# Narrow feed-forwards of a one-core transformer pair: order of one weight split, place of the rotary tables, and a first weight chunk handled in halves

## The reference, cut to what matters

```python
def rmsnorm(x, g):                      # x * rsqrt(mean(x*x) + eps) * g
def swiglu(x, w_gate, w_up, w_down):
    return (jax.nn.silu(x @ w_gate) * (x @ w_up)) @ w_down
for i in range(DEPTH):                  # DEPTH = 2
    h = h + 0.5 * swiglu(rmsnorm(h, ffn1_norm[i]), ffn1_w_gate[i], ffn1_w_up[i], ffn1_w_down[i])
    ...                                 # a mixer: latent attention with rotary angles, an mLSTM, a Fourier mixer
    h = h + 0.5 * swiglu(rmsnorm(h, ffn2_norm[i]), ffn2_w_gate[i], ffn2_w_up[i], ffn2_w_down[i])
    ...                                 # a gated embedding
```

## Time and profile before

| what | us |
|---|---|
| timed runs: median (lowest, highest) | 3465.66 (3457.43, 3468.33) |
| profiled execution: its own time | 3451.29 |
| span of the profile | 3449.5 |
| TensorE busy in the span | 3305.6 (96%) |
| mean granted TensorE clock | 0.976 of full speed |

### The profile page before, as it was taken

One profiled execution on the slowest core, in us unless ns is written; L12 is line 12 of the kernel. 1 busy time (PEld: TensorE's weight loads), 2 busy tenths in 40 slices (PEclk: granted clock), 3 DMA queues, 4 the chain that ended last, 5 costly groups with the idle time before them and its releaser, 6 DMA issues. The chain is left out here.

```text
span 3449.5 us, 56469 instructions
## 1 busy us (share of the span) xinstructions
PE 3305.6 (96%) x23726; PEld 2867.6 (83%) x23726; DVE 1565.9 (45%) x2285; ACT 1226.2 (36%) x1823; POOL 53.8 (2%) x67
## 2 busy tenths in 40 slices
PE   7999999999999989999999899999999999997899
PEld 7997899999779978888788888758888788875799
DVE  5544464654445542223674556532233323346444
ACT  4333334443333452223543333332223322233333
POOL 0000000000000000000000000000000000000000
PEclk9999999999999989999999999999999999999999
DMA  6446544454655422222223222122222222220353
GB/s 239 167 148 230 207 173 160 180 183 154 237 184 183 170 99 96 97 98 85 98 86 120 102 99 97 54 86 97 93 90 97 86 97 95 88 74 25 110 183 122
DMA packets 62913, 439.21 MB, mean 127 GB/s; under 512 B 6672, under 2 KB 9872, under 8 KB 10000
## 3 DMA queue, kind: packets, MB, share of 16 engines
q1 hardware_dynamic: 61552, 435.43, 34.8%
q10 hardware_dynamic: 1184, 1.18, 0.1%
HBM read 435.53 MB, written 1.05 MB: 127 GB/s over the span
## 5 line engine op out<-in xcount | busy, mean ns | idle before, releaser
L641 ACT ACTIVATE sb_w_split<-sb_ring 128x2048 fp32r<-128x2048 f32 x264 | 505.2, 1914 | 1041.8 <-PE ps_low L458 854.3
L649 DVE TENSOR_TENSOR sb_w_split<-sb_ring,sb_w_split 128x2048 fp32r<-128x2048 f32 x264 | 604.5, 2290 | 543.2 <-ACT sb_w_split L641 543.2
L458 PE MATMUL ps_low<-sb_x_split,sb_w_split 128*128 128x256 f32 (+1 forms) x4224 | 706.3, 328 | 36.9 <-DVE sb_w_split L649 25.9
L458 PEld LDWEIGHTS ps_low<-sb_x_split,sb_w_split 128*128 128x128 f32 x4224 | 630.6, 194 | 102.6 <-issue 21.7
L458 PE MATMUL ps_high<-sb_x_split,sb_w_split 128*128 128x256 f32 (+1 forms) x4224 | 690.2, 323 | 0.5 <-DVE sb_w_split L649 0.5
L458 PEld LDWEIGHTS ps_high<-sb_x_split,sb_w_split 128*128 128x128 f32 x4224 | 618.1, 190 | 62.4 <-DVE sb_w_split L649 0.7
L458 PE MATMUL ps_low<-sb_a_split,sb_w_split 128*128 128x256 f32 (+1 forms) x2112 | 372.0, 326 | 12.9 <-DVE sb_arena L1142 9.0
L458 PE MATMUL ps_high<-sb_a_split,sb_w_split 128*128 128x256 f32 (+1 forms) x2112 | 369.1, 324 | 0.0
L458 PEld LDWEIGHTS ps_low<-sb_a_split,sb_w_split 128*128 128x128 f32 x2112 | 314.7, 191 | 52.3 <-issue 14.4
L458 PEld LDWEIGHTS ps_high<-sb_a_split,sb_w_split 128*128 128x128 f32 x2112 | 315.3, 191 | 30.4
L458 PE MATMUL ps_low<-sb_xn,sb_ring 128*128 128x256 f32 (+1 forms) x800 | 186.8, 392 | 1.8 <-ACT sb_xn L2264 1.8
(11 more groups left out here) (316 smaller groups left out, 3100.0 us busy)
## 6 DMA issues: line engine op xcount, KB each, us to landing
sb_ring<-weights SPq DMA_DIRECT2D x411, 1024.0 KB, 4.8
sb_consts<-consts SPq DMA_DIRECT2D x1, 2017.0 KB, 13.8
sb_h<-xT SPq DMA_DIRECT2D x1, 1024.0 KB, 5.8
sb_h<-ctxT ACTq DMA_DIRECT2D x1, 1024.0 KB, 17.3
out<-sb_h SPq DMA_DIRECT2D x1, 1024.0 KB, 4.8
sb_vectors<-vectors SPq DMA_DIRECT2D x1, 269.0 KB, 2.8
sb_arena<-positions ACTq DMA_DIRECT2D x1, 128.0 KB, 7.2
```

The costliest lines, as they stand in the source:

```text
L458: ins = self.g.nc.tensor.matmul(out, lhsT, rhs, start=start, stop=stop)
L641: g.nc.scalar.activation(g.w_split[:, 0, s % 2, :], g.ring[:, n % SLOTS, :], ACT.Copy).then_inc(g.sem["w_high"], 1)
L649: g.nc.vector.tensor_tensor(g.w_split[:, 1, s % 2, :], g.ring[:, n % SLOTS, :], g.w_split[:, 0, s % 2, :].bitcast(F32), ALU.subtract).then ...
```

## The change

In all four narrow feed-forwards the split of chunk 4 moves ahead of the first silu (ACT) and between the first gates and the first products (DVE). In the first one, the rotary tables move from ahead of the last pair to behind the last split of the down chunks. At the start of the program ACT gets a Square of one column that waits only for the constant eps; and chunk 0 is split in two halves of 1024 columns (row tiles k = 0 to 3 and 4 to 7 of the weights), for which TensorE waits separately.

```diff
+def first_split(g, half):
+    cols = slice(half * CHUNK // 2, (half + 1) * CHUNK // 2)
+    return g.w_split[:, 0, 0, cols], g.w_split[:, 1, 0, cols], g.ring[:, 0, cols]
+
+def first_split_high(act):
+    g = act.g
+    act.wait_ge(g.landed[0], 16)
+    for half in range(2):
+        high, _, whole = first_split(g, half)
+        name = "w_high" if half else "first_high"
+        g.nc.scalar.activation(high, whole, ACT.Copy).then_inc(g.sem[name], 1)
+
+def first_split_low(dve):
+    g = dve.g
+    for half in range(2):
+        high, low, whole = first_split(g, half)
+        dve.wait_ge(g.sem["w_high" if half else "first_high"], 1)
+        g.nc.vector.tensor_tensor(low, whole, high.bitcast(F32), ALU.subtract).then_inc(g.used[0] if half else g.sem["first_low"], 1)
...
 def first_gates():        # in plain_ffn_tensor
+        first = kind == "ffn1" and l == 0
+        if first:
+            pe.wait_ge(g.sem["first_low"], 1)
...
         for k in range(KT):
+            if first and k == KT // 2:
+                pe.wait_ge(g.used[0], 1)
...
 # plain_ffn_scalar
     plain_root_scalar(act, others=2)
-    silu(0)
-    silu(1)
-    pair(1)
+    split_high(act, 4)
+    for f in range(4):
+        silu(f)
+    split_high(act, 5)
     with act.engine.Fori(0, (PAIRS_FF - 3) // 2) as it:
         for p in range(2, 4):
             pair(p, it)
-    if kind == "ffn1" and l == 0:
-        setup_scalar(act)
...
     with act.engine.Fori(0, 2) as it:
         for c in range(1, 5):
             ahead(c, it)
+    if kind == "ffn1" and l == 0:
+        setup_scalar(act)
...
 # plain_ffn_vector
     scaled_gate(0)
     scaled_gate(1)
+    split_low(dve, 4)
     product(0)
     product(1)
-    pair(1)
+    scaled_gate(2)
+    scaled_gate(3)
+    product(2)
+    product(3)
+    split_low(dve, 5)
...
-    if kind == "ffn1" and l == 0:
-        setup_vector(dve)
...
     with dve.engine.Fori(0, 2) as it:
         for c in range(1, 5):
             ahead(c, it)
+    if kind == "ffn1" and l == 0:
+        setup_vector(dve)
...
 # start of the ACT program
+            act.wait_ge(g.sem["vec_step"], 1)
+            g.nc.scalar.activation(g.root[:, 0:1], g.eps[:, 0:1], ACT.Square).then_inc(g.sem["act_step"], act.adds("act_step"))
             act.wait_ge(g.sem["vectors_in"], act.due("vectors_in", 16))
...
-                                 between=lambda j: split_high(act, 0) if j == 3 else None)
+                                 between=lambda j: first_split_high(act) if j == 3 else None)
...
 # start of the DVE program
                 if j == 3:
-                    split_low(dve, 0)
+                    first_split_low(dve)
```

More of the change, by code:

```diff
@@ L349 @@
     "x_in", "ctx_in", "pos_in", "ple_in",
-    "w_high",
+    "w_high", "first_high", "first_low",
     "split_used",
@@ L987, in first_gates @@
     def first_gates():
-        w = [part.rearrange("p (k n) -> p k n", k=KT) for part in weights(0)]
+        first = kind == "ffn1" and l == 0
+        if first:
+            pe.wait_ge(g.sem["first_low"], 1)
+            w = [g.w_split[:, part, 0, :] for part in range(2)]
+        else:
+            w = weights(0)
+        w = [part.rearrange("p (k n) -> p k n", k=KT) for part in w]
         for f in range(2):
```

## The result

| kernel | median us | lowest to highest | executions |
|---|---|---|---|
| before | 3465.77 | 3455.52 to 3469.44 | 12 |
| changed | 3446.74 | 3438.09 to 3454.83 | 12 |

The ratio is 0.9946, 95% interval 0.9935 to 0.9957: 18.7 us faster, between 14.9 and 22.5. The forecast was 3440.5 us and a gain of 25.1; the time lies in the range, but the gain falls short of the forecast by 6 us, and 25.1 lies outside the interval. The profiled execution of the changed kernel took 3447.47 us (span 3445.7), only 3.8 less than that of before.

A forecast was written before the change was run, and what follows sets the result against it. TensorE, busy 96%, was taken to bound the kernel, so only its waits and the slow clock behind them counted: 3.2 + 15.2 + 6.7 = 25.1 us off the median 3465.66 gives 3440.5 us, range 3431 to 3452.

The forecast's parts named there:

- The start: Program start: early table load and chunk 0 in halves bring TensorE's first matmul from 15.45 to 12.25, gain 3.2 us.
- The landing of chunk 0: Program start: chunk 0's load lands at 9.5 us, 0.4 ahead of ACT's need at 9.90.
- Chunk 4: Four narrow feed-forwards: the wait and slow clock at chunk 4 go, net 3.8 us each, 15.2 in all.
- The new wait at chunk 5: Narrow feed-forwards: chunk 5 can start at 46.6, chunk 4 ends at 46.4; a new wait of some 0.3 us.
- The rotary tables: First feed-forward, ahead of the down chunks: 4.5 us of wait and the rest slow clock go, gain 6.7 us.
- the sum: Whole kernel: 3.2 + 15.2 + 6.7 = 25.1 us, taken as a shift off the median 3465.66, giving 3440.5 us.
- rival B: Feed-forwards: the stall moves from chunk 4 to chunk 5, wait 2.5 us; gain 9.9, time 3455.8 us; chance 0.08.
- A: Program start: loads of chunk 0 or later chunks hold TensorE back; gain 21.9, time 3443.8 us; chance 0.15.
- D: Program start: the table load still comes behind xT; gain 23.8, time 3441.8 us; chance 0.74 together with the forecast.
- C: Feed-forward loop: the new order starts a lag each pair keeps, costing 51.8 us, time 3492 us; chance 0.03.

The follow-up runs named there:

- e1: The kernel before with only the early one-column Square and chunk 0 in halves; ratio 1.0000 (0.9990 to 1.0011).
- e9: The changed kernel with the start of before, so only the chunk 4 move and the rotary move; ratio to before 0.9962 (0.9948 to 0.9977).
- e2: The kernel before with only chunk 4's split moved ahead of the silus in four feed-forwards; ratio 0.9978 (0.9965 to 0.9991).
- e6: The kernel before with six unused fp32 matmuls filling TensorE's wait ahead of chunk 4 in four feed-forwards; ratio 1.0011 (0.9999 to 1.0022).
- e7: A repeat of e2, only chunk 4's split moved, against the kernel before; ratio 0.9975 (0.9963 to 0.9988).
- e8: The kernel before with four unused fp32 matmuls (1.8 us) once between chunks 0 and 1 of the first feed-forward; ratio 0.9984 (0.9974 to 0.9994).
- e3: The kernel before with only the rotary tables moved behind the last split; ratio 0.9965 (0.9951 to 0.9979).
- e10: The changed kernel with two unused matmuls (0.9 us) between chunks 0 and 1 of the first feed-forward; ratio to before 0.9942 (0.9927 to 0.9957).
- e11: The changed kernel with four unused matmuls (1.8 us) between chunks 0 and 1 of the first feed-forward; ratio to before 0.9943 (0.9927 to 0.9958).

## Why the prediction was right or wrong

**The start, 3.2 us: right in the mechanism and, from xT on, in the size.** The table load left the path, both halves cost about what the like operations elsewhere cost (1.99 us for the two high parts, 2.38 for the two low parts), no drain of 1.4 us showed behind the load (0.75 + 1.28 = 2.03, the ACTIVATE starts at 2.04), and nothing behind was late. The landing of chunk 0, taken as fixed at 9.5, moves with that of xT, and the first matmul came at 14.06, not near 12.3, for that reason alone. Chunk 0 runs in part at the lower clock and takes 8.19 us instead of 7.61, so chunk 1 follows xT by 22.08 - 8.85 = 13.2 us instead of 22.89 - 7.05 = 15.8, 2.6 earlier; but that is a draw and not a cost of the step: with this start chunk 0 took 7.40 in e1, where chunk 1 follows xT by 12.4, and with the old start it took up to 8.57 (e9). Alone it is worth nothing that can be measured (e1); that e9 lacks some 5 us of the changed kernel's gain is within the two intervals.

**Chunk 4, 3.8 us each: right locally.** Measured 15.64 - 11.66 = 4.0 and 15.57 - 11.73 = 3.8. The new wait at chunk 5 that was forecast at 0.3 is 45.68 - 39.78 - 5.76 = 0.14.

**The rotary tables, 6.7 us: right locally**, 19.53 - 12.93 = 6.6; the adds began late and TensorE did not notice, as worked out.

**The step that failed is the sum**, though the time came out inside the range. It failed in the words "the gain is a shift of everything behind it, so I take it off the median". The waits are such a shift: 3.2 + 4 x 2.4 + 4.5 = 17.3 us, and the full-speed equivalent fell by 15.8 and 17.0. The clock's part of the terms, 4 x 1.6 behind chunk 4 and 2.1 ahead of the down chunks, some 8 us, was taken from the same rows and is not a shift: the time at half clock of the whole program is 178.0 ± 2.7 and 180.3 ± 7.1 us after, 181.5 ± 2.1 before, where about 2 x 8 = 16 less would have followed (an estimate: half of the time at half clock is lost). Other falls came in place of those that were removed, in the mixers by what the profiles show: that of layer 0 takes 5 to 8 us longer in both profiles of the changed kernel, that of layer 1 takes 1.1 and 7.6 longer than in the first of before. Waits alone would have given a forecast of 17, against 18.7 (14.9 to 22.5) measured. That 3446.74 lies in the range of 3431 to 3452 is owed to the room left for the scatter of medians and for rival B: the gains of 20 to 26.5 alone reached up to 3446.

**The rivals.** A (the loads hold the start back) and D (the table load stays) did not happen in any profile, nor did B (the stall moves to chunk 5) or C (a lag in the loop: the loop's chunks are 5.76 apart as before). The offset of the one profiled execution from the median, 14.4 us, was rightly not carried into the forecast, but it was mostly a draw of the clock and should have warned of the terms that were read from that execution's clock.

**What stays open.** Shown are that local clock savings did not arrive in the total (e2, e6, e7, e9), that the mixer of layer 1 is longer in each profile without the fall at chunk 4, and that a short delay changes the time at half clock (e8). What decides where in the mixers the clock falls was not found, nor why those mixers' own waits grow in some profiles. The total does not come back to one figure: it is 167 us in e3, e10 and e11, 171 in e8, 191 in e6 and 193 in e1. That a fixed amount is conserved is not shown.

## What to carry to other kernels

Count a removed TensorE wait at its own length (here the full-speed equivalent followed that within 2.5 us). Do not add the slow matmuls behind it as a gain, even when they are in the trace every time, as long as the program has other places where the clock falls; they can come back there. To compare two kernels that differ by less than 1%, use many executions and split each into its full-speed equivalent and its time at half clock: the first is sharp (errors of 0.3 to 0.8 us here, and some 0.8 us for each 10 us at half clock by which the two kernels differ), the second carries most of the scatter, and a single profile can be 14 us off by it.

## What the runs showed of the hardware that was not expected

- Filling TensorE's wait with useless matmuls kept the clock up there (chunk 4 in 6.01 us instead of 7.38) and brought nothing in all (1.0011).
- A delay of 1.8 us at the start made the whole faster, by 5.5 us (2.1 to 9.0).
- Each profile without the clock's fall at chunk 4 has a longer mixer of layer 1, 175.7 to 185.2 us instead of 174.0 to 174.7, in code that is the same.
- The input xT, issued at 1.2 us in each, was usable between 6.97 and 8.92 us in 14 profiles; the first matmul follows it at a fixed distance, 8.40 us with the old start and 5.20 or 5.21 with the new one.
- An ACT_TABLE_LOAD in front of an ACTIVATE that waits for xT did not run ahead of that wait; with a one-column ACTIVATE put first it ran at 0.75 us, ahead even of the instruction that sets that ACTIVATE's operand (0.81).
